# Two transformer blocks in split fp32r on one core: weight blocks woven in pairs and read with a step of two, even and odd tokens as stationary blocks

## The chip, the cores and the metric

The kernel runs on one core of one Trainium2 chip. The metric is device time in microseconds (us) of one execution; it ran three times, in 753.06, 753.13 and 756.38 us, median 753.13 us.

## What is computed

A sequence of 256 tokens of width 1024 goes through two different blocks, all in float32. The first block: an RMS norm and an input projection to 4608 columns, a gated causal convolution with 31 taps and one with 3 taps, two output projections joined by sigmoid gates, a projection back, a feed-forward part (up to 2 x 2816 columns, 3-tap convolution, gelu, product, down to 1024) and a gated embedding branch. The second block: two kinds of attention over 256 tokens, then

```
h = rms_norm(x, ffn_pre_g)
u = h @ w_up                      # 1024 x 8192
c = 3-tap causal convolution of u over tokens, plus bias
g, val = split(c)
o = (gelu(g) * val) @ w_down      # 4096 x 1024
x = x + rms_norm(o, ffn_post_g)
```

Some 134 MB of weights are read from HBM once each.

## The kernel before

**Split products.** Every weight and every activation is held as two fp32r tiles, a rounded part (`hi`) and the rest (`lo`). A product of two of them is three matmuls: hi x hi, lo x hi, hi x lo. Each matmul takes a stationary operand of 128 partitions x 128 columns, which a weight load (PEld in the profile) puts into the array first, and streams a moving operand past it.

**Units.** A weight matrix comes in units of 8 blocks (the first down projection 11, one small projection 4), each block 128 x 128, lying side by side in a partition: block k is `[:, k*P:(k+1)*P]`, 128 adjacent floats. SyncE loads a unit (512 KB, line 564) into one of four `raw` buffers, ScalarE rounds it to `w_hi` (L787), VectorE (L1223) or, for some units, GpSimd (L636) writes `w_lo`, and TensorE consumes it. Buffers rotate with a ring of four; work on a unit is done up to three units ahead. The order on every engine is written out by hand.

**TensorE.** `products` (L1895 to L1906) multiplies all blocks of a unit. Three lines hold nearly all of the work: L1901 (`w_hi` stationary, hi part of the activation moving), L1902 (`w_hi` again, lo part) and L1903 (`w_lo`, hi part). The moving operand is `hi[:, k, :]`, 256 tokens in adjacent floats. `lagging` (L1914, L1915, L1920) and the second input unit (L2017, L2018, L2021) do the same in another order. Each of the three matmuls has a weight load of its own.

The second down projection (`down2`, L2347 to L2349, `token_products`) is the other way round: the stationary operand is a block of 128 tokens of `f_hi` or `f_lo`, and 512 weight columns stream past:

```
to, tok = o_tile(half, b)[:], slice(b * P, (b + 1) * P)
cols = slice(first_col(u) + j * HALF, first_col(u) + (j + 1) * HALF)
wh, wl = (w[slot(u)][:, cols] for w in (w_hi, w_lo))
nc.tensor.matmul(to, f_hi[:, k, tok], wh, start=start, stop=False)
nc.tensor.matmul(to, f_lo[:, k, tok], wh, start=False, stop=False)
return nc.tensor.matmul(to, f_hi[:, k, tok], wl, start=False, stop=stop)
```

`first_col(u)` is 0 for the first three units of `down2` and 8 from the fourth on: from there the weights lie 32 bytes later in their buffers, and nothing else about the matmuls differs.

**Other matmuls.** L2287 and L2293 transpose `X` and `branch` (stationary, 128 x 128) against the identity. L1959 sums squares with one moving column. L2217 to L2220 multiply attention probabilities with 64 moving columns. L2076 streams 256 columns of `ones_over` past blocks of `conv`, in plain float32.

**VectorE in the second up projection** (`up2`, 64 units). For each unit it does `feed_forward`'s share: a scaling of the bank (L1281), two taps of the convolution (L1572), one of L1590 (`src`) and L1562 (`f_lo`) in turn, and the `w_lo` of a later unit, except for every fourth unit, which GpSimd splits.

**The step before `up2`.** `scale_branch` (L1780) multiplies a chunk of `branch`, 128 x 256, by a per-token factor in a PSUM bank, into `tmp`; the sum with `X` follows, and ScalarE squares it (L811) and rounds it (L814).

Of the kernel before, what the change touches and what calls it, by code (L numbers as in the profile page):

```python
# [20 lines left out]
P = 128  # L21
TOK = 256
D = 1024
DC = D // P
# [8 lines left out]
HALF = D // 2  # L33
# [245 lines left out]
def build(nc, d):  # L279
    f32, f32r = mybir.dt.float32, mybir.dt.float32r  # L280
    ALU, ACT, AX = mybir.AluOpType, mybir.ActivationFunctionType, mybir.AxisListType
    ds = bass.ds

    with ExitStack() as ctx:
# [18 lines left out]
        ident = sb("ident", [P, P])  # L303
# [28 lines left out]
        h2_hi, h2_lo = sb("h2_hi", [P, DC, TOK], f32r), sb("h2_lo", [P, DC, TOK], f32r)  # L332
# [108 lines left out]
        def o_tile(half, b):  # L441

            return bank[UP2_BANKS[2 * half + b]]
# [91 lines left out]

        def slot(u):
            return u % RING

        def on_side(u):
            return u - UNIT0["out2"] in OUT2_SIDE  # L540
# [674 lines left out]
        def _(dve):  # L1215
# [561 lines left out]

            def scale_branch(c):

                nc.vector.tensor_tensor(tmp[c % 4][:], branch[:, c, :], rbc[:, 0:TOK], ALU.mult  # L1780
                                        ).then_inc(res_step, 1)

            for c in range(1 + len(OUT2_SIDE), DC - 2):
# [98 lines left out]
        def _(pe):  # L1882
# [7 lines left out]
            def unit_here(u, it=0):  # L1890
                pe.wait_ge(lo_ready[slot(u)], it + (u // RING + 1))

            def products(ps, s, block0, ks, hi, lo, start, stop, ready=None, w=None):

                w_of = w or (w_hi[s], w_lo[s])  # L1895
                for n, k in enumerate(ks):
                    if ready is not None:
                        pe.wait_ge(*ready(k))
                    b = block0 + n
                    wh, wl = (part[:, b * P:(b + 1) * P] for part in w_of)  # L1900
                    nc.tensor.matmul(ps, wh, hi[:, k, :], start=start and n == 0, stop=False)  # L1901
                    nc.tensor.matmul(ps, wh, lo[:, k, :], start=False, stop=False)  # L1902
                    last = nc.tensor.matmul(ps, wl, hi[:, k, :], start=False,  # L1903
                                            stop=stop and n == len(ks) - 1)
                return last

            def lagging(tiles, ks, hi, lo, hi_here, lo_here, start, stop):

                for k in list(ks) + [None]:
                    if k is not None:  # L1910
                        pe.wait_ge(*hi_here(k))
                        for ps, s in tiles:
                            wh, wl = (part[s][:, k * P:(k + 1) * P] for part in (w_hi, w_lo))
                            nc.tensor.matmul(ps, wh, hi[:, k, :], start=start and k == ks[0], stop=False)  # L1914
                            nc.tensor.matmul(ps, wl, hi[:, k, :], start=False, stop=False)  # L1915
                    if k != ks[0]:
                        behind = ks[-1] if k is None else k - 1
                        pe.wait_ge(*lo_here(behind))
                        for ps, s in tiles:
                            last = nc.tensor.matmul(ps, w_hi[s][:, behind * P:(behind + 1) * P],  # L1920
                                                    lo[:, behind, :], start=False,
                                                    stop=stop and k is None)
                            if stop and k is None:
                                last.then_inc(unit_done, 1)
# [13 lines left out]
            def mean_squares(name):  # L1938

                col = ones_over[:, 0:1] if name == "ln" else ones_over[:, P:P + 1]  # L1940
                parts = ["final", "final_g"] if name == "final" else [name]
                chunks = CK if name == "ln" else DC
                sums = (sumsq,) if name in ALL_ADDED or name == "final" else (sumsq, last_sq)
                if name == "in":
                    sums = (sumsq[:, 0:1, :], sumsq[:, 1:2, :])
                    pe.wait_ge(sum_ready, ADD["in", DC - 2])
                elif name == "up2":
                    sums = (sumsq[:, 0:1, :], sumsq[:, 1:2, :])
                    pe.wait_ge(pair_sum, DC // 2 - 1)
                elif name == "final":  # L1950
                    pe.wait_ge(last_added, 1)
                else:
                    pe.wait_ge(sum_ready, ADD[parts[-1], chunks - len(sums)])
                for n in range(len(parts)):
                    for b in range(2):
                        for k, part in enumerate(sums):
                            if part is last_sq and b == 0:
                                pe.wait_ge(sq_ready, SQ[parts[n], chunks - 1])
                            last = nc.tensor.matmul(stat_of(name)[:, 2 * n + b:2 * n + b + 1],  # L1959
                                                    part[:, n, b * P:(b + 1) * P], col,  # L1960
                                                    start=k == 0, stop=k == len(sums) - 1)
                last.then_inc(stat_ready, 1)

# [48 lines left out]
            def rounded_first(u):  # L2012

                ps = in_tile(u)
                for k in range(DC):
                    wh = w_hi[slot(u)][:, k * P:(k + 1) * P]
                    nc.tensor.matmul(ps, wh, h2_hi[:, k, :], start=k == 0, stop=False)  # L2017
                    nc.tensor.matmul(ps, wh, h2_lo[:, k, :], start=False, stop=False)  # L2018
                unit_here(u)
                for k in range(DC):  # L2020
                    last = nc.tensor.matmul(ps, w_lo[slot(u)][:, k * P:(k + 1) * P], h2_hi[:, k, :],  # L2021
                                            start=False, stop=k == DC - 1)
                last.then_inc(unit_done, 1)

            for u in range(24):
# [11 lines left out]
                first = 0  # L2037
# [87 lines left out]
            def down_tile(name, i, t, it, per_tile, ready=None):  # L2125

                k = BLOCKS[name]
                for r in range(per_tile):
                    u = UNIT0[name] + per_tile * i + r
                    unit_here(u, it)  # L2130
                    if r == 0:
                        if isinstance(it, int):
                            bank_free(t)
                        else:
                            bank_free(t, it, 2 if per_tile == 2 else 1)
                    products(bank[slot(t)][:, 0:TOK], slot(u), 0, range(k * r, k * r + k),
                             f_hi, f_lo, r == 0, r == per_tile - 1, ready).then_inc(unit_done, 1)

            for i in range(DC):
                down_tile("down", i, TILE0["down"] + i, 0, 2, chunk_ready("f") if i == 0 else None)  # L2140
# [143 lines left out]
            def x_transposes(b):  # L2284

                for c in range(DC):
                    last = nc.tensor.transpose(xT_ps[b][c // 4][:, c % 4 * P:(c % 4 + 1) * P],  # L2287
                                               X[:, c, b * P:(b + 1) * P], ident[:])
                last.then_inc(xT_done, 1)

            def branch_transposes(b, first, end):
                for c in range(first, end):
                    last = nc.tensor.transpose(branch_ps[b][c // 4][:, c % 4 * P:(c % 4 + 1) * P],  # L2293
                                               branch[:, c, b * P:(b + 1) * P], ident[:])
                if end == DC:
                    last.then_inc(branchT_done, 1)

# [43 lines left out]

            def token_products(half, b, u, j, k, start, stop):

                to, tok = o_tile(half, b)[:], slice(b * P, (b + 1) * P)
                cols = slice(first_col(u) + j * HALF, first_col(u) + (j + 1) * HALF)
                wh, wl = (w[slot(u)][:, cols] for w in (w_hi, w_lo))
                nc.tensor.matmul(to, f_hi[:, k, tok], wh, start=start, stop=False)  # L2347
                nc.tensor.matmul(to, f_lo[:, k, tok], wh, start=False, stop=False)  # L2348
                return nc.tensor.matmul(to, f_hi[:, k, tok], wl, start=False, stop=stop)  # L2349
# [32 lines left out]
def units_of(w, k_blocks, order=None):  # L2382


    K, N = w.shape
    t = w.reshape(K // P, P, N // P, P).transpose(2, 0, 1, 3)
    if order is not None:
        t = t[order]
    t = t.reshape(-1, k_blocks, P, P).transpose(0, 2, 1, 3)
    return t.reshape(-1, P, k_blocks * P)  # L2390


# [69 lines left out]
```

## Time and profile before

| | |
|---|---|
| median of three executions | 753.13 us (753.06 to 756.38) |
| span of the profiled execution | 753.8 us; its page gives no other time of its own |
| TensorE matmul / weight load | 744.0 us (99%) / 723.4 us (96%), 5950 of each |
| VectorE | 577.9 us (77%) |
| ScalarE | 452.2 us (60%) |
| GpSimd | 210.7 us (28%) |
| HBM read | 133.80 MB, 179 GB/s over the span |

Busy times count every instant at which at least one instruction of that engine is under way. Matmuls are pipelined: several are under way at once and their ends are modelled, so the distance between two starts says more than the duration of one. PEld is the weight load, which overlaps the matmul before it. Starts are in us from the start of the span. A row with xN merges N instructions of one line: its second number reaches from the first start to the last end.

### The profile page before, as it was taken

To read this page: it belongs to the slowest core of one execution; us is meant where nothing else is said; L and a number is where in the kernel's file an instruction comes from. 1 tells how busy PE (TensorE), PEld (TensorE's weight loads), DVE (VectorE), ACT (ScalarE), POOL (GpSimd) and SP (SyncE) were. 2 spreads that over 40 slices of the span, in tenths; PEclk is the share of its full clock that TensorE was granted. 3 is DMA by queue.
4 is the path that set the end of the run, shared out by engine and by line. 5 is a ranking of instruction groups with operands and counts; after the bars stand their busy time and mean duration, and the time that the engine had idled before them with its cause. 6 is when DMAs were issued, how large, how long until landed. Compare 5 with 4: busy or idle time off the path is not lost.

```text
span 753.8 us, 16764 instructions
## 1 busy us (share of the span) xinstructions
PE 744.0 (99%) x5950; PEld 723.4 (96%) x5950; DVE 577.9 (77%) x1049; ACT 452.2 (60%) x765; POOL 210.7 (28%) x136
## 2 busy tenths in 40 slices
PE   8999999999999999999999999999999999999997
PEld 8999999999999999999999999899999999988885
DVE  6999977877887887434887794899999999973333
ACT  7645555556665665444765697876766666643431
POOL 0476743460000000343464002422122122212220
PEclk9999999999999999999999999999999999999999
DMA  8575644565555567644443333355565555666551
GB/s 313 177 238 178 196 155 137 188 207 190 189 184 182 191 200 246 204 161 141 163 165 130 124 130 128 107 195 196 195 194 184 182 192 192 205 217 195 184 179 56
DMA packets 37917, 135.48 MB, mean 180 GB/s; under 512 B 4464, under 2 KB 4720, under 8 KB 37872
## 3 DMA queue, kind: packets, MB, share of 16 engines
q1 hardware_dynamic: 37728, 134.86, 54.3%
q8 instruction: 30, 0.49, 0.3%
q14 instruction: 15, 0.12, 0.1%
q10 hardware_dynamic: 144, 0.00, 0.0%
HBM read 133.80 MB, written 1.05 MB: 179 GB/s over the span
## 4 chain that ended last, share of the span: by engine, by line
PE 72%; DVE 5%; ACT 3%; issue 2%; POOL 1%; DMA 1%; DVEq 0%; POOLq 0%; SPq 0%; ACTq 0%
PE bank L1901 20%; PE bank L1903 19%; PE bank L1902 19%; PE bank L2348 4%; PE bank L2347 4%; PE bank L2349 4%; DVE w_lo L1223 2%; ACT w_hi L787 1%; DMA raw<-in_w_o 1%; POOL X L755 1%; PE bank L2176 1%; ACT score L1079 0%; PE bank L2200 0%; DVE sumsq L1813 0%; DVE score L1730 0%
## 5 line engine op out<-in xcount | busy, mean ns | idle before, releaser
L1901 PE MATMUL bank<-h_hi,w_hi 128*128 128x256 f32 x1372 | 386.6, 282 | 1.6 <-DVE h_lo L1235 0.8
L1902 PE MATMUL bank<-h_lo,w_hi 128*128 128x256 f32 x1372 | 383.4, 279 | 0.0
L1903 PE MATMUL bank<-h_hi,w_lo 128*128 128x256 f32 x1372 | 382.6, 279 | 0.0
L787 ACT ACTIVATE w_hi<-raw 128x1024 fp32r<-128x1024 f32 (+2 forms) x243 | 258.6, 1067 | 94.3 <-PE bank L1903 42.4
L1223 DVE TENSOR_TENSOR w_lo<-raw,w_hi 128x1024 fp32r<-128x1024 f32 (+2 forms) x187 | 235.9, 1264 | 88.4 <-ACT w_hi L787 86.4
L1901 PEld LDWEIGHTS bank<-h_hi,w_hi 128*128 128x128 f32 x1372 | 257.8, 188 | 3.2 <-DVE w_lo L1301 1.0
L1902 PEld LDWEIGHTS bank<-h_lo,w_hi 128*128 128x128 f32 x1372 | 257.9, 188 | 0.0
L1903 PEld LDWEIGHTS bank<-h_hi,w_lo 128*128 128x128 f32 x1372 | 257.9, 188 | 0.0
L636 POOL TENSOR_TENSOR w_lo<-raw,w_hi 128x1024 fp32r<-128x1024 f32 (+1 forms) x56 | 139.0, 2485 | 384.8 <-ACT w_hi L787 376.3
L1281 DVE TENSOR_TENSOR bank<-bank,scales 128x256 f32<-128x256 f32 x116 | 49.4, 429 | 27.4 <-PE bank L1903 21.0
L1572 DVE SCALAR_TENSOR_TENSOR cg<-bank,vec,cg 128x255 f32<-128x255 f32 x108 | 51.2, 474 | 0.7 <-ACT cg L1019 0.6
L2347 PE MATMUL bank<-w_hi,f_hi 128*128 128x512 f32 x128 | 49.9, 390 | 0.0
L2349 PE MATMUL bank<-w_lo,f_hi 128*128 128x512 f32 x128 | 49.9, 390 | 0.0
L2348 PE MATMUL bank<-w_hi,f_lo 128*128 128x512 f32 x128 | 49.9, 390 | 0.0
L1901 PE MATMUL bank<-f_hi,w_hi 128*128 128x256 f32 x176 | 49.5, 281 | 0.0
L1902 PE MATMUL bank<-f_lo,w_hi 128*128 128x256 f32 x176 | 49.3, 280 | 0.0
L1903 PE MATMUL bank<-f_hi,w_lo 128*128 128x256 f32 x176 | 48.9, 278 | 0.0
L649 POOL TENSOR_TENSOR sumsq<-sq,sumsq 128x256 f32<-128x256 f32 x33 | 34.3, 1046 | 52.1 <-ACT sq L811 51.6
L1337 DVE SCALAR_TENSOR_TENSOR conv<-bank,vec,conv 128x256 f32<-128x256 f32 x120 | 48.3, 472 | 0.0
L1562 DVE TENSOR_TENSOR f_lo<-src,f_hi 128x256 f32 (+1 forms) x54 | 42.8, 793 | 0.5 <-ACT f_hi L970 0.5
L970 ACT ACTIVATE f_hi<-src 128x256 f32 (+1 forms) x54 | 22.2, 412 | 31.9 <-DVE src L1590 31.9
L1019 ACT ACTIVATE cg<-bank,vec 128x256 f32<-128x256 f32 x54 | 30.6, 566 | 16.7 <-DVE bank L1281 15.2
(235 smaller groups left out, 948.6 us busy)
## 6 DMA issues: line engine op xcount, KB each, us to landing
raw<-in_w_up SPq DMA_DIRECT2D x108, 512.0 KB, 4.2
raw<-in_w_in SPq DMA_DIRECT2D x53, 512.0 KB, 3.9
raw<-in_w_down SPq DMA_DIRECT2D x32, 512.0 KB, 4.2
raw<-in_w_down SPq DMA_DIRECT2D x16, 704.0 KB, 4.1
raw<-in_w_o SPq DMA_DIRECT2D x8, 512.0 KB, 4.6
raw<-in_w_gate SPq DMA_DIRECT2D x8, 512.0 KB, 3.3
raw<-in_w_out SPq DMA_DIRECT2D x8, 512.0 KB, 3.3
raw<-in_w_b_out SPq DMA_DIRECT2D x4, 512.0 KB, 3.5
```

The costliest lines, as they stand in the source:

```text
L636: nc.gpsimd.tensor_tensor(w_lo[s][:, cols], raw[s][:, cols], w_hi[s][:, cols].bitcast(f32), ALU.subtract).then_inc(lo_ready[s], 1)
L787: nc.scalar.activation(hi_of(u)[:, cols], raw[s][:, cols], ACT.Copy).then_inc(hi_ready, 1)
L1223: nc.vector.tensor_tensor(lo_of(u)[:, cols], raw[s][:, cols], hi_of(u)[:, cols].bitcast(f32), ALU.subtract).then_inc(lo_ready[s], 1)
L1281: nc.vector.tensor_tensor(tile, tile, scales[:, 0, :], ALU.mult).then_inc(scaled, 1)
L1337: nc.vector.scalar_tensor_tensor(conv[:, i, :], a_pad[i][:, tap:tap + TOK], w, conv[:, i, :], ALU.mult, ALU.add).then_inc(conv_step, 1)
L1572: nc.vector.scalar_tensor_tensor(c[:, k:TOK], source[:, 0:TOK - k], vcol(w, 3 * col + (2 - k)), c[:, k:TOK], ALU.mult, ALU.add).then_inc(t ...
L1901: nc.tensor.matmul(ps, wh, hi[:, k, :], start=start and n == 0, stop=False)
L1902: nc.tensor.matmul(ps, wh, lo[:, k, :], start=False, stop=False)
L1903: last = nc.tensor.matmul(ps, wl, hi[:, k, :], start=False, stop=stop and n == len(ks) - 1)
L2347: nc.tensor.matmul(to, f_hi[:, k, tok], wh, start=start, stop=False)
L2348: nc.tensor.matmul(to, f_lo[:, k, tok], wh, start=False, stop=False)
L2349: return nc.tensor.matmul(to, f_hi[:, k, tok], wl, start=False, stop=stop)
```

## The change

Three things change, all of them in how data lies and is addressed. (1) On the host, the blocks of a unit are woven in pairs: blocks 2i and 2i+1 share 256 floats, one in the even places, the other in the odd ones. A stationary operand is then read with a step of two floats over 256 of them. The eleventh block of a unit of the first down projection stays as it was. (2) In `down2`, the two stationary token blocks are the even and the odd tokens in place of the first and the last 128, read from `f_hi` and `f_lo` with a step of two; transposes of `X` and `branch` and the sum of squares ahead of them take their tokens alike, `scale_branch` spreads its factor over the tokens in that order, and the host puts the output rows back in order. (3) Nothing else: the number, the order, the waits and the sizes of the instructions are the same on every engine (the listings of both kernels' instruction orders agree row by row but for line numbers: 3639 rows of TensorE, 625 of VectorE, 536 of ScalarE, 122 of GpSimd, 156 of SyncE). The addresses at which buffers begin are the same too.

```
+        def stationary(tile, k, blocks=DC):
+            if k + 1 == blocks and blocks % 2:
+                return tile[:, k * P:(k + 1) * P]
+            first = k // 2 * 2 * P + k % 2
+            return tile[:, first:first + 2 * P - 1:2]
+
+        def tokens_of(b):
+            return slice(b, TOK - 1 + b, 2)
...
-                nc.vector.tensor_tensor(tmp[c % 4][:], branch[:, c, :], rbc[:, 0:TOK], ALU.mult
+                nc.vector.tensor_tensor(tmp[c % 4][:].rearrange("p (t b) -> p t b", b=2),
+                                        branch[:, c, :].rearrange("p (t b) -> p t b", b=2),
+                                        rbc[:, 0:TOK].rearrange("p (b t) -> p t b", b=2), ALU.mult
                                         ).then_inc(res_step, 1)
...
-                    wh, wl = (part[:, b * P:(b + 1) * P] for part in w_of)
+                    wh, wl = (stationary(part, b, blocks) for part in w_of)
                     nc.tensor.matmul(ps, wh, hi[:, k, :], start=start and n == 0, stop=False)
                     nc.tensor.matmul(ps, wh, lo[:, k, :], start=False, stop=False)
...
-                to, tok = o_tile(half, b)[:], slice(b * P, (b + 1) * P)
+                to, tok = o_tile(half, b)[:], tokens_of(b)
                 cols = slice(first_col(u) + j * HALF, first_col(u) + (j + 1) * HALF)
...
     t = t.reshape(-1, k_blocks, P, P).transpose(0, 2, 1, 3)
-    return t.reshape(-1, P, k_blocks * P)
+    count, pairs = t.shape[0], k_blocks // 2
+    woven = t[:, :, :2 * pairs].reshape(count, P, pairs, 2, P).swapaxes(3, 4)
+    return np.concatenate([woven.reshape(count, P, -1), t[:, :, 2 * pairs:].reshape(count, P, k_blocks % 2 * P)], axis=2)
```

`lagging`, the second input unit, the transposes (L2287, L2293) and the sum of squares of the step before `up2` get the same replacement of their stationary slice.

## Rows read from the trace of the kernel before

**Rows 1.** The page: header, busy times, chain that ended last.

```profile
span 753.8 us, 16764 instructions
PE 744.0 (99%) x5950; PEld 723.4 (96%) x5950; DVE 577.9 (77%) x1049; ACT 452.2 (60%) x765; POOL 210.7 (28%) x136
...
PE bank L1901 20%; PE bank L1903 19%; PE bank L1902 19%; PE bank L2348 4%; PE bank L2347 4%; PE bank L2349 4%; DVE w_lo L1223 2%; ACT w_hi L787 1%; DMA raw<-in_w_o 1%; POOL X L755 1%; PE bank L2176 1%; ACT score L1079 0%; PE bank L2200 0%; DVE sumsq L1813 0%; DVE score L1730 0%
```

**Rows 2.** Matmuls in order of time, first up projection, then `up2`: first and last of 31.

```profile
300.20 0.28 PE L1901 MATMUL bank<-f_hi,w_hi 128*128 128x256 f32 x1
...
303.73 0.28 PE L1901 MATMUL bank<-f_hi,w_hi 128*128 128x256 f32 x1
...
600.02 0.28 PE L1902 MATMUL bank<-h_lo,w_hi 128*128 128x256 f32 x1
...
603.52 0.28 PE L1902 MATMUL bank<-h_lo,w_hi 128*128 128x256 f32 x1
```

**Rows 3.** Matmuls of `down2` in order of time, around the fourth unit's first (669.21).

```profile
667.81 0.40 PE L2347 MATMUL bank<-w_hi,f_hi 128*128 128x512 f32 x1
...
669.21 0.40 PE L2347 MATMUL bank<-w_hi,f_hi 128*128 128x512 f32 x1
...
671.93 0.39 PE L2347 MATMUL bank<-w_hi,f_hi 128*128 128x512 f32 x1
```

**Rows 4.** Weight loads in order of time, those of L2076 and of L1959.

```profile
106.78 1.49 PEld L2076 LDWEIGHTS bank<-conv,ones_over 128*128 128x128 f32 x7
...
15.32 0.86 PEld L1959 LDWEIGHTS bank<-ones_over,sumsq 128*128 128x128 f32 x7
```

**Rows 5.** Matmuls in order of time: eight transposes of `X`.

```profile
473.42 1.04 PE L2287 MATMUL bank<-ident,X 128*128 128x128 f32 x8
```

**Rows 6.** Groups by line and shape: counts and mean duration.

```profile
L1901 PE MATMUL bank<-h_hi,w_hi 128*128 128x256 f32 x1372 | 386.6, 282 | 1.6 <-DVE h_lo L1235 0.8 <-DVE h_lo L1524 0.5 <-DVE w_lo L1223 0.2
L1901 PE MATMUL bank<-f_hi,w_hi 128*128 128x256 f32 x176 | 49.5, 281 | 0.0
L2347 PE MATMUL bank<-w_hi,f_hi 128*128 128x512 f32 x128 | 49.9, 390 | 0.0
L2076 PEld LDWEIGHTS bank<-conv,ones_over 128*128 128x128 f32 x8 | 1.4, 190 | 0.2
```

**Rows 7.** Busy time of each engine in stretches (columns as the last query names them).

```profile
core 0: us, PE busy (x) PEld busy (x) DVE busy (x) ACT busy (x) POOL busy (x), PEclk, DMA share, GB/s
550.00:650.00 100.00, 100.00 (x860) 100.00 (x859) 96.65 (x170) 67.26 (x108) 21.68 (x9) 1.00 0.58 193
...
105.00:150.00 45.00, 44.51 (x370) 43.88 (x369) 32.53 (x59) 25.14 (x42) 18.12 (x9) 1.00 0.47 154
385.00:470.00 85.00, 84.71 (x721) 81.75 (x720) 62.25 (x145) 61.16 (x163) 24.09 (x25) 1.00 0.40 134
470.00:494.00 24.00, 22.68 (x190) 21.75 (x189) 17.96 (x33) 20.11 (x40) 11.68 (x11) 1.00 0.39 129
```

**Rows 8.** VectorE in `up2`, in order of time.

```profile
565.81 0.43 DVE L1281 TENSOR_TENSOR bank<-bank,scales 128x256 f32<-128x256 f32 x1
...
568.01 0.48 DVE L1572 SCALAR_TENSOR_TENSOR cg<-bank,vec,cg 128x254 f32<-128x254 f32 x1
568.61 0.43 DVE L1281 TENSOR_TENSOR bank<-bank,scales 128x256 f32<-128x256 f32 x1
...
569.34 1.74 DVE L1562 TENSOR_TENSOR f_lo<-src,f_hi 128x256 f32 x1
...
571.41 0.43 DVE L1281 TENSOR_TENSOR bank<-bank,scales 128x256 f32<-128x256 f32 x1
```

**Rows 9.** Chain of waits between the convolutions and the projection back.

```profile
129.10 5.95 DMA raw<-in_w_o
```

**Rows 10.** VectorE just before `up2`, in order of time.

```profile
481.91 0.41 DVE L1780 TENSOR_TENSOR tmp<-branch,bank 128x256 f32<-128x256 f32 x1
...
482.79 0.41 DVE L1780 TENSOR_TENSOR tmp<-branch,bank 128x256 f32<-128x256 f32 x1
```

More of the change, by code:

```diff
@@ L1891, in unit_here, with products @@
                 pe.wait_ge(lo_ready[slot(u)], it + (u // RING + 1))
-            def products(ps, s, block0, ks, hi, lo, start, stop, ready=None, w=None):
+            def products(ps, s, block0, ks, hi, lo, start, stop, ready=None, w=None, blocks=DC):
                 w_of = w or (w_hi[s], w_lo[s])
@@ L1912, in lagging @@
                         for ps, s in tiles:
-                            wh, wl = (part[s][:, k * P:(k + 1) * P] for part in (w_hi, w_lo))
+                            wh, wl = (stationary(part[s], k) for part in (w_hi, w_lo))
                             nc.tensor.matmul(ps, wh, hi[:, k, :], start=start and k == ks[0], stop=False)
@@ L1919, in lagging @@
                         for ps, s in tiles:
-                            last = nc.tensor.matmul(ps, w_hi[s][:, behind * P:(behind + 1) * P],
+                            last = nc.tensor.matmul(ps, stationary(w_hi[s], behind),
                                                     lo[:, behind, :], start=False,
@@ L1959, in mean_squares @@
                             last = nc.tensor.matmul(stat_of(name)[:, 2 * n + b:2 * n + b + 1],
-                                                    part[:, n, b * P:(b + 1) * P], col,
+                                                    part[:, n, tokens_of(b) if name == "post" else slice(b * P, (b + 1) * P)], col,
                                                     start=k == 0, stop=k == len(sums) - 1)
@@ L2015, in rounded_first @@
                 for k in range(DC):
-                    wh = w_hi[slot(u)][:, k * P:(k + 1) * P]
+                    wh = stationary(w_hi[slot(u)], k)
                     nc.tensor.matmul(ps, wh, h2_hi[:, k, :], start=k == 0, stop=False)
@@ L2020, in rounded_first @@
                 for k in range(DC):
-                    last = nc.tensor.matmul(ps, w_lo[slot(u)][:, k * P:(k + 1) * P], h2_hi[:, k, :],
+                    last = nc.tensor.matmul(ps, stationary(w_lo[slot(u)], k), h2_hi[:, k, :],
                                             start=False, stop=k == DC - 1)
@@ L2136, in down_tile @@
                     products(bank[slot(t)][:, 0:TOK], slot(u), 0, range(k * r, k * r + k),
-                             f_hi, f_lo, r == 0, r == per_tile - 1, ready).then_inc(unit_done, 1)
+                             f_hi, f_lo, r == 0, r == per_tile - 1, ready, blocks=k
+                             ).then_inc(unit_done, 1)
             for i in range(DC):
@@ L2287, in x_transposes @@
                     last = nc.tensor.transpose(xT_ps[b][c // 4][:, c % 4 * P:(c % 4 + 1) * P],
-                                               X[:, c, b * P:(b + 1) * P], ident[:])
+                                               X[:, c, tokens_of(b)], ident[:])
                 last.then_inc(xT_done, 1)
@@ L2293, in branch_transposes @@
                     last = nc.tensor.transpose(branch_ps[b][c // 4][:, c % 4 * P:(c % 4 + 1) * P],
-                                               branch[:, c, b * P:(b + 1) * P], ident[:])
+                                               branch[:, c, tokens_of(b)], ident[:])
                 if end == DC:
@@ L2459 @@
     r = run_bass_kernel_spmd(nc, [{f"in_{k}": v for k, v in arrays.items()}], core_ids=[0])
-    out = r.results[0]["out"].reshape(2, 2, P, HALF).transpose(0, 2, 1, 3)
+    out = r.results[0]["out"].reshape(2, 2, P, HALF).transpose(2, 0, 1, 3)
     return np.ascontiguousarray(out).reshape(1, TOK, D)
```

## The prediction

> **What bounds the kernel now.** I read the page first. TensorE has a matmul under way 99% of the span and a weight load 96% of it, and the chain that ended last lies on L1901 to L1903 and L2347 to L2349 with 70% [rows 1]. The next engine, VectorE, is at 77%. TensorE hardly waits for anyone, so its time is the number of matmuls times the distance between their starts. That distance is what the reader is to look at, in the rows in order of time.
>
> In the first up projection 30 matmuls of 256 columns take 303.73 - 300.20 = 3.53 us, 117.7 ns each; in `up2` they take 3.50 us, 116.7 ns each [rows 2]. In `down2` six matmuls of 512 columns take 1.40 us, 233.3 ns each, up to 669.21, and from there twelve take 2.72 us, 226.7 ns each [rows 3]. [...]
>
> [...]
>
> [...]
>
> [...] The rows show that the distance depends on an address alone, 233.3 against 226.7 ns [rows 3]. [...]
>
> **512 columns.** 384 matmuls, three lines of 128 [rows 6]. [...] I take 216. The first three units are 36 matmuls: 36 x 17.3 = 0.6 us. The other 348 give 348 x 10.7 = 3.7 us. Together 4.3 us.
>
> **256 columns.** Lines L1901 to L1903 hold 1372 + 176 matmuls each of the two large groups [rows 6], and with the smaller groups of the same shape 1692 each; L1914, L1915, L1920 add 44 each and the second input unit 24: 5232 in all. 48 of them (the eleventh blocks) keep their step of one, worth 0.3 us, neglected. About 280 us of the span run at 116.7 ns, 2400 matmuls, and 2832 run at 117.7. To what do they fall? [...] But a load cannot follow the last at any distance: where only one column streams, the loads of L1959 are (0.86 - 0.19)/6 = 0.112 us apart [rows 4]. The transposes' 0.110 is nearly that. I take 111.7, because the loads of the split products are of L1959's kind, not transposes. Gain: 2832 x 6.0 + 2400 x 5.0 = 29.0 us. With 109.7 it would be 2832 x 8.0 + 2400 x 7.0 = 39.5 us. Both ends are kept for the range.
>
> **Does the next engine let it?** In `up2` VectorE is busy 96.65 of 100 us [rows 7]. For a unit it needs, from start to start, 568.01 + 0.40 - 565.81 = 2.6 us and then idles until the bank comes (568.61); in the unit that GpSimd splits, the write of `f_lo` takes 1.74 us beside it and the unit takes 571.41 - 568.61 = 2.80 us without a gap [rows 8]. Four units: 3 x 2.6 + 2.8 = 10.6 us. TensorE needs 4 x 24 x 116.7 = 11.2 us now, 4 x 24 x 111.7 = 10.7 at my value and 10.5 at 109.7. So at 111.7 VectorE just keeps up; at 109.7 it would be the bound and take back 16 x 0.1 = 2 us, and some more for its late start into `up2`. ScalarE (67%) and the DMA engines (58%) have room [rows 7].
>
> **What is given back.** Three stretches are paced by other engines too. From 105 to 150 the chain runs through VectorE and a transfer of `raw<-in_w_o` of 5.95 us [rows 9]; 370 matmuls there [rows 7] would give 2.1 us, and I count half lost, 1.0. From 470 to 494 ScalarE and VectorE feed TensorE chunk by chunk (PE 22.68 of 24 us, 190 matmuls): 1.0 us, all lost. In attention, 385 to 470, 721 matmuls would give 4 us at most; ScalarE and VectorE are at 72 and 73% with serial steps, and I count a third lost, 1.2. The start of the input projection, where split weights are ready less than 1 us ahead, may cost 0.5. Together 3.7 us.
>
> **`scale_branch`.** Its row takes 0.41 us, and eight of them stand in the chain before `up2`, about 0.88 us apart [rows 10]. Now the factor is read from PSUM in two places in turn, and the output is the same size. No row has such a read. It can cost nothing (same elements) or double, 8 x 0.41 = 3.3 us. I take nothing, as nearest to the many rows of two-operand work at about 0.42 us, and keep 3.3. The stepped transposes and sums are 36 matmuls, and I count nothing for them: their loads are hidden in the same way.
>
> **The sum.** 29.0 + 4.3 - 3.7 = 29.6 us. The profiled execution's span is 753.8 us, 0.7 above the median of 753.13, so I take the gain off the median: **723 us**, 4% faster. This case's own range is 715 to 733.
>
> **Rivals.**
>
> *The load has no floor at 111.7.* Then matmuls of 256 columns fall to 109.7 and VectorE bounds `up2`. Gain 39.5 + 4.3 - 2 - 5 (more is lost in the three stretches) = 37 us: 716. For it: the transposes. Chance 0.15.
>
> *Half of the surcharge stays.* [...] Gain (29.0 + 4.3)/2 - 2 = 15: 738. Chance 0.14.
>
> *Nothing moves.* [...] 753, or up to 756 with `scale_branch`. [...] Chance 0.10.
>
> *The load becomes the slower read.* [...] It decides from the point where a stepped load takes over 117 ns; at 125 ns the kernel would need 5232 x 8 = 42 us more. Chance 0.16. [...]
>
> **Chances and range.** The forecast has 0.45. About half a per cent (4 us) is what a measurement of this kernel can tell from no change. Faster by more: 0.45 + 0.15 + 0.14 = 0.74. Within: 0.10. Slower: 0.16. From 708 (the lower rival with nothing lost, 753.1 - 44) to 755 holds the forecast, both other gains and most of no change, 0.81.
>
> **What the changed profile would show.** Starts of the split products 111 to 113 ns apart in both up projections, with no difference left between them; `down2` at 216 ns, the first three units like the rest. PEld about 188 ns per load as before. VectorE near 100% in `up2`, waiting for ScalarE or TensorE hardly at all. The forecast is wrong if the distance stays over 115 ns, if loads take longer than 190 ns, if `down2` gains and the 256-column products don't (then a load's floor decides), or if TensorE shows idle time in `up2` before L1223's `w_lo`.

## The result, and the profile after

The change makes the kernel slower. Four executions took 772.80 to 774.18 us, median **773.65 us**; the kernel before took 753.23 us beside them, so the ratio is 1.026 (95% interval 1.025 to 1.0276). The forecast was 723 us, and its range ended at 755.

The page of the kernel after, header and busy times, stands against [rows 1]:

```profile
span 771.8 us, 16764 instructions
PE 764.1 (99%) x5950; PEld 744.4 (96%) x5950; DVE 578.8 (75%) x1049; ACT 452.3 (59%) x765; POOL 210.0 (27%) x136
```

The span grew by 18.0 us; TensorE grew by 20.1 and its load side by 21.0, with the same 5950 instructions. The busy times of VectorE, ScalarE and GpSimd did not move by a microsecond. TensorE does not wait longer either: its waits were 3.8 us in seven places before and are 1.8 us in two now. So only the distance between two matmuls is left. Here it is in order of time, for the input projection, the first up projection, `up2` and `down2` (start, duration):

```profile
29.73 0.28 PE L1914 MATMUL bank<-h_hi,w_hi 128*128 128x256 f32 x1
...
33.69 0.28 PE L1914 MATMUL bank<-h_hi,w_hi 128*128 128x256 f32 x1
...
299.94 0.28 PE L1914 MATMUL bank<-f_hi,w_hi 128*128 128x256 f32 x1
...
303.93 0.28 PE L1914 MATMUL bank<-f_hi,w_hi 128*128 128x256 f32 x1
...
599.83 0.28 PE L1915 MATMUL bank<-h_lo,w_hi 128*128 128x256 f32 x1
...
603.83 0.28 PE L1915 MATMUL bank<-h_lo,w_hi 128*128 128x256 f32 x1
...
719.98 0.39 PE L2361 MATMUL bank<-w_hi,f_hi 128*128 128x512 f32 x1
...
722.78 0.39 PE L2361 MATMUL bank<-w_hi,f_hi 128*128 128x512 f32 x1
```

The first three pairs lie 33 matmuls apart: 3.96, 3.99 and 4.00 us, 120.0, 120.9 and 121.2 ns each, where [rows 2] had 117.7 and 116.7. The last pair lies 12 apart: 233.3 ns, where [rows 3] had 226.7 from the fourth unit on. That is the whole difference: 5184 stepped matmuls of 256 columns from 117.2 to 120.6 ns (the means over the long stretches before and after) are 17.6 us, and 348 of 512 columns from 226.7 to 233.3 are 2.3 us, together 19.9 of the 20.4 us between the medians.

Groups of the kernel after, by line and shape:

```profile
L1914 PE MATMUL bank<-h_hi,w_hi 128*128 128x256 f32 x1372 | 392.4, 286 | 0.1
L1914 PEld LDWEIGHTS bank<-h_hi,w_hi 128*128 128x128 f32 x1372 | 269.9, 197 | 1.2 <-issue 0.2 <-DVE w_lo L1234 0.2
L1791 DVE TENSOR_TENSOR tmp<-branch,bank 128x256 f32<-128x256 f32 x8 | 3.3, 412 | 1.2 <-PE bank L1984 1.2
```

A load takes 197 ns in place of 188; loads above 190 ns were one of the signs that the prediction had named for itself being wrong. `scale_branch` takes 0.41 us as before [rows 10]. In `up2` VectorE is busy 92.9 of 100 us in place of 96.65 [rows 7]: it had room, and the wait was TensorE's own pace.

### The profile page after: what moved, and what is told of

Same layout as the page of the kernel before. It is cut to its first block, busy times and chain, and to the rows that moved or that the text cites. A ratio compares the mean times of both kernels' runs of the same rounds, so it can differ in the third digit from the quotient of the medians.

```text
span 771.8 us, 16764 instructions
## 1 busy us (share of the span) xinstructions
PE 764.1 (99%) x5950; PEld 744.4 (96%) x5950; DVE 578.8 (75%) x1049; ACT 452.3 (59%) x765; POOL 210.0 (27%) x136
## 4 chain that ended last, share of the span: by engine, by line
PE 95%; POOL 1%; DVE 1%; issue 1%; DMA 1%; ACT 0%; SPq 0%; DVEq 0%; POOLq 0%
PE bank L1914 27%; PE bank L1915 26%; PE bank L1916 26%; PE bank L2362 4%; PE bank L2363 4%; PE bank L2361 4%; PE bank L2190 1%; DMA raw<-in_w_in 1%; POOL X L766 1%; PE bank L2214 1%; PE bank L1972 1%; PE bank L2232 0%; PE bank L2234 0%; PE bank L1927 0%; PE bank L1933 0%
## 5 line engine op out<-in xcount | busy, mean ns | idle before, releaser
L1914 PE MATMUL bank<-h_hi,w_hi 128*128 128x256 f32 x1372 | 392.4, 286 | 0.1
L1915 PE MATMUL bank<-h_lo,w_hi 128*128 128x256 f32 x1372 | 389.5, 284 | 0.0
L1916 PE MATMUL bank<-h_hi,w_lo 128*128 128x256 f32 x1372 | 389.5, 284 | 0.0
L1914 PEld LDWEIGHTS bank<-h_hi,w_hi 128*128 128x128 f32 x1372 | 269.9, 197 | 1.2 <-issue 0.2
L1915 PEld LDWEIGHTS bank<-h_lo,w_hi 128*128 128x128 f32 x1372 | 269.9, 197 | 0.0
L1916 PEld LDWEIGHTS bank<-h_hi,w_lo 128*128 128x128 f32 x1372 | 269.8, 197 | 0.0
L1030 ACT ACTIVATE cv<-bank,vec 128x256 f32<-128x256 f32 x32 | 18.1, 566 | 40.0 <-DVE bank L1292 40.0
```

Of the source, the lines that this page charges most:

```text
L1030: nc.scalar.activation((cg if r == 0 else cv)[q][:], ff_tile(name, n, turn), ACT.Identity, bias=vcol(b, col), scale=vcol(w, 3 * col + 2)). ...
L1916: last = nc.tensor.matmul(ps, wl, hi[:, k, :], start=False, stop=stop and n == len(ks) - 1)
```

## The experiments

That the distances would fall to 111.7 and 216 ns rested on a supposition of the author that no row shows: that the weight load's read and the stream's read hold each other up where they meet, and that equal pace would end the meetings. Below, the surcharge is what a matmul takes above those two values. Against it stood the theory that the load's own read becomes the slow one. A third possibility was that only the position of the two operands counts. The matmuls had to be measured by themselves first.

### Trains of matmuls by themselves: loads_measured, loads_measured_2

These kernels leave the whole computation of the blocks out. Each line issues 48 matmuls back to back, from tiles whose offsets are known to the byte:

```
+ for n in range(48): nc.tensor.matmul(ps[n % 2][:, 0:256], st(n, 2, 0), mv(n, 256), start=True, stop=True)
  # st(n, step, offset): 128 floats of block n % 8; mv(n, columns): the moving operand
```

> Not the model but 30 trains of 48 split-product matmuls on two fp32r tiles (its output is a copy of weights, the block's computation is left out). Theory A (a weight load has a floor of its own that rises with the step, 112 ns at a step of one and 120 ns at two, because the load touches more memory lines): with 64 moving columns, where only the load counts, the distances are 112 ns at step one, 120 ns at step two and more at four; with 256 moving columns step two gives 120 ns at every offset; with 512 step two is 227 to 233 ns. Theory B (the load itself keeps 112 ns, and the two reads collide): with 64 columns steps one and two give the same 112 ns, and with 256 columns step two falls to 112 ns at some of the four offsets. With the moving operand held at one address (step zero) theory B expects no surcharge in either case, theory A 120 ns at step two.

> Again trains of 48 matmuls and no block computation, now with 256-column trains between the short ones to hold the clock. Theory A2 (each of the two reads has a pace limit of its own, set by the 16-byte pieces it touches; a 512-column stream and a stepped load are both at it and each pays its surcharge by itself): with the stream held at one address, 512 columns are about 216 ns apart at step one and step two alike; with the load held at one address or on one block, they stay at 227 to 234 ns. With 128 moving columns the distance is 112 ns at step one, 118 to 120 at two, about 173 at three and 233 at four. Theory B (the surcharge is made by the two reads meeting): holding either read at one address takes it away, 216 ns in all these trains, and 128 columns give 112 ns at steps one and two. The table of offsets of 256-column trains: A2 expects 116 to 120 ns in every cell, no cell at 112.

The distance in a train is (duration of the row - duration of one matmul)/47. One matmul takes 0.22 us with 128 columns, 0.28 with 256 and 0.39 with 512, and 0.40 where its load is slow (steps of four and eight). The rows are rounded to 0.01 us, which makes 0.2 ns of the distance. Matmuls of the first kernel in order of time. 256 columns: L69 has loads with a step of two, L81 to L83 of three, four and eight, L84 loads of one address. 512 columns: L73 a step of one, L77 of two, L85 one address:

```profile
51.51 5.93 PE L69 MATMUL ps<-mov,sta 128*128 128x256 f32 x48
...
74.59 11.06 PE L73 MATMUL ps<-mov,sta 128*128 128x512 f32 x48
...
119.11 11.36 PE L77 MATMUL ps<-mov,sta 128*128 128x512 f32 x48
...
163.68 8.43 PE L81 MATMUL ps<-mov,sta 128*128 128x256 f32 x48
171.94 11.37 PE L82 MATMUL ps<-mov,sta 128*128 128x256 f32 x48
183.15 11.74 PE L83 MATMUL ps<-mov,sta 128*128 128x256 f32 x48
194.73 5.61 PE L84 MATMUL ps<-mov,sta 128*128 128x256 f32 x48
200.18 11.26 PE L85 MATMUL ps<-mov,sta 128*128 128x512 f32 x48
```

Beside 256 columns a load with a step of two costs 120 ns at all four offsets tried (120.0 to 120.9). A step of three costs 173 ns, of four 233, of eight 241: from four on it costs hardly more. Four floats are 16 bytes. With steps of 2, 3, 4 and 8, 128 floats touch 64, 96, 128 and 128 pieces of 16 bytes, and the distances are 1.88, 1.81, 1.82 and 1.89 ns per piece. From a step of two on, the price goes by pieces, not by bytes. With a step of one it does not: 32 pieces take 112 ns at least (below).

The trains of 64 columns that were to separate the theories in this kernel can't do it. TensorE's granted clock was 0.98 while it streamed 64 columns beside loads of step one, and 0.50 in the two trains behind, so that step one and step two ran at different clocks. The train with a step of four took 233 ns there too (L88, 11.37 us for the 48, clock 0.50): half the clock did not slow it.

Matmuls of the second kernel in order of time. 512 columns: L65 and L66 stream one address, L65 with a load step of one and L66 of two, L67 loads one address, L68 loads one block again and again. 256 columns: L69 loads one address; L71 and L72 stream one address, L71 with a load step of one, L72 of two. 128 columns: L73 a step of one, L75 of two:

```profile
29.42 10.66 PE L65 MATMUL ps<-mov,sta 128*128 128x512 f32 x48
39.92 10.66 PE L66 MATMUL ps<-mov,sta 128*128 128x512 f32 x48
50.41 11.15 PE L67 MATMUL ps<-mov,sta 128*128 128x512 f32 x48
61.40 11.07 PE L68 MATMUL ps<-mov,sta 128*128 128x512 f32 x48
72.31 5.76 PE L69 MATMUL ps<-mov,sta 128*128 128x256 f32 x48
...
83.66 5.54 PE L71 MATMUL ps<-mov,sta 128*128 128x256 f32 x48
89.04 5.82 PE L72 MATMUL ps<-mov,sta 128*128 128x256 f32 x48
94.69 5.47 PE L73 MATMUL ps<-mov,sta 128*128 128x128 f32 x48
...
105.73 5.76 PE L75 MATMUL ps<-mov,sta 128*128 128x128 f32 x48
```

The pair L71, L72 separates the theories. The stream reads one address, so that by the supposition nothing is left to meet, and the stepped load still needs 117.9 ns where the plain one needs 111.9. With 128 columns it is the same: 111.7 and 117.9. **A stepped load has a floor of its own at 118 ns.** (The trains of 128 columns with steps of three and four ran in part at a lower granted clock, 0.79 and 0.64, and are left aside.)

The floor is not the whole loss. In the kernel the distance went from 117.2 to 120.6 ns; a floor of 117.9 forbids any gain, but by itself asks for only 0.7 ns more, 3.6 of the 17.6 us. The rest appears only when both reads move: a stepped load takes 120.0 to 120.9 ns beside a real stream and 117.9 beside one address, a plain one 117.2 to 120.0 and 111.9. For 512 columns the floor can't be the cause at all, for it lies 100 ns below the distance. With the stream at one address both steps take the same 218.5 ns (L65, L66); with a real stream, operands level, a step of one takes 227.0 and a step of two 233.4 (L73, L77 above). That is something the two reads do to each other, and no run says what.

The other surprise is the stream. With the load at one address, 512 columns still take 229 to 231 ns (L67 here, L85 above); with the stream at one address they take 218.5. So most of what 512 columns take above the forecast's 216 ns belongs to the stream: 512 adjacent fp32r columns are 128 pieces too, at 1.77 to 1.81 ns each. With 256 columns and the load at one address, 113.4 (L84 above) to 116.6 ns (L69 here) are left.

A last table of the second kernel varies the two offsets in steps of 32 bytes, modulo 128, at 256 columns and a step of one. Level operands take 119.8 to 120.0 ns in all four cases. Operands apart mostly take 117.9 to 118.7, with one exception at 119.8, (stationary 0, moving 96), and one at 113.4, (64, 0). With 512 columns level is the good place, 227.0 to 227.4; apart, they take 229.1 to 234.3 in both kernels. So position counts as well.

So the larger part of the surcharge of 512 columns does not depend on where the load reads, since it stays with the load at one address (229 ns, L67). The rest depends on both reads: the same matmul of 256 columns takes 113.4 to 120.0 ns by position alone, and the step of the load moves the distance of 512 columns by 6 ns (227.0 in L73, 233.4 in L77), though the load's own floor of 118 ns lies far below it.

### The two halves of the change: weights_only, tokens_only

The first kernel keeps the woven weights alone, the second the even and odd tokens alone.

```
weights_only                                      tokens_only
 def tokens_of(b):                                 def stationary(tile, k, blocks=DC):
-    return slice(b, TOK - 1 + b, 2)              -    first = k // 2 * 2 * P + k % 2
+    return slice(b * P, (b + 1) * P)             -    return tile[:, first:first + 2 * P - 1:2]
                                                  +    return tile[:, k * P:(k + 1) * P]
```

> Only the woven weight blocks; token blocks as before. Theory A: 256-column matmuls 120 to 121 ns apart, 512-column ones 227 and 233 as before: 753 + 5232 x 3.4 ns = 771 us. Theory C (the loss comes from the stepped token blocks, transposes and scale_branch, with the weights neutral): 753 us.

> Only even and odd tokens as stationary blocks, weights as before. Theory A: 256-column matmuls 116.7 and 117.7 ns apart as before, 512-column ones 233 ns throughout, 348 x 6.6 ns = 2.3 us more, and some tenths for transposes and scale_branch: 755.5 to 756 us. Theory C: 770 us or more.

`weights_only` took 770.98 us, ratio 1.0235 (1.0221 to 1.0249), and `tokens_only` 755.86 us, 1.0036 (1.0022 to 1.005). 17.7 and 2.6 us make up the 20.4. Matmuls of `down2` in order of time, 12 apart in the first kernel and 9 in the second:

```profile
700.19 0.39 PE L2359 MATMUL bank<-w_hi,f_hi 128*128 128x512 f32 x1
...
702.91 0.39 PE L2359 MATMUL bank<-w_hi,f_hi 128*128 128x512 f32 x1
```

```profile
699.77 0.39 PE L2358 MATMUL bank<-w_hi,f_hi 128*128 128x512 f32 x1
...
701.87 0.39 PE L2358 MATMUL bank<-w_hi,f_hi 128*128 128x512 f32 x1
```

226.7 ns with whole token blocks, 233.3 with stepped ones: each half of the change pays where its own loads are. In `tokens_only` the matmuls of 256 columns lie 116.7 ns apart everywhere, also in the first up projection, where the profiled run of the kernel before had 117.7 [rows 2], though nothing differs there. That ns can come and go without an edit.

### A step of four in the kernel: weights_step4

```
-            first = k // 2 * 2 * P + k % 2
-            return tile[:, first:first + 2 * P - 1:2]
+            first = k // 4 * 4 * P + k % 4
+            return tile[:, first:first + 4 * P - 3:4]
```

> Weight blocks woven in fours, read with a step of four (the last three blocks of a unit of the first down projection with a step of one): 5088 of the 5232 split matmuls of 256 columns. Theory A2: their load takes 233 ns as in the trains with a step of four, so 5088 x (233.3 - 117.2) = 591 us more, about 1344 us. Theory B, equal pace being what counts: a step of four runs twice as fast as the stream, the mirror image of the kernel before, and costs about as much as that one, 753 to 790 us.

It took 1343.1 us, ratio 1.779 (1.774 to 1.784). The token blocks are those of the kernel before. The weights are woven in fours, 5088 of the 5232 matmuls read them so, and the three blocks left over of a unit of eleven keep a step of one. Matmuls in order of time, where such a unit passes from the one to the other:

```profile
566.12 0.40 PE L1913 MATMUL bank<-f_lo,w_hi 128*128 128x256 f32 x1
566.36 0.40 PE L1914 MATMUL bank<-f_hi,w_lo 128*128 128x256 f32 x1
566.59 0.28 PE L1912 MATMUL bank<-f_hi,w_hi 128*128 128x256 f32 x1
566.71 0.28 PE L1913 MATMUL bank<-f_lo,w_hi 128*128 128x256 f32 x1
566.83 0.28 PE L1914 MATMUL bank<-f_hi,w_lo 128*128 128x256 f32 x1
```

235 ns, then 120: the price hangs on the load of each matmul by itself. 5088 x (233.3 - 117.2) = 591 us, and 588 were measured (the kernel before took 754.8 us beside it). By the theory that an unequal pace makes meetings and nothing else counts, a step of four would have cost at most a few dozen us; it is ruled out.

### Position in the kernel: ring_at_0, ring_at_64, step2_ring_at_0

In the kernel before, activations begin 64 bytes and weight buffers 32 bytes past a multiple of 128. These three move buffers and change nothing else (in `ring_at_0`, `o_ms` and `o_rstd` share a tile, and the shift in `down2` is 64 bytes).

```
-RING_PAST = 32
+RING_PAST = 64                                   # ring_at_0; ring_at_64: 0
-        w_hi = [sb(f"w_hi{i}", [P, UNIT_MAX], f32r, past=RING_PAST) for i in range(RING)]
+        w_hi = [sb(f"w_hi{i}", [P, UNIT_MAX], f32r) for i in range(RING)]
...                                               # raw and w_lo alike
+        at[0] += 64                              # ring_at_0 only
```

> The kernel before with its weight buffers 32 bytes lower, at 0 in place of 32 modulo 128 bytes, so that blocks of weights and activations stand 64 bytes apart modulo 128 (before: 96); the weights of the second down projection from its fourth unit on stand level with the tokens as before. The trains found 113.3 ns or 117.8 ns at a distance of 64. Theory A2 with the meeting of reads as a second, smaller term: 113.3 ns wherever the good pattern locks in, down to 753 - 5232 x 3.9 ns = 733 us; if the other locks in, 117.8 ns and 754 to 756 us. A theory without any effect of position: 753 us.

> The kernel before with its weight buffers at 64 modulo 128, level with the activations. All trains at a distance of 0 gave 120.0 ns: 753 + 5232 x 2.8 ns = 768 us by the trains, with the 512-column matmuls at 226.7 ns in all units. Without any effect of position: 753 us.

> The changed kernel (step of two in weights and tokens) with the weight buffers at 0 modulo 128. Theory A2: the stepped load sets 120 ns wherever it stands, 771 to 774 us as without the shift. If the stepped load only lost by standing badly to the stream: 753 us or less.

`ring_at_64` puts both operands level and took 768.81 us, 1.0197 (1.0182 to 1.0212). Its `up2` in order of time, 30 matmuls, 120.0 ns each:

```profile
599.90 0.28 PE L1901 MATMUL bank<-h_hi,w_hi 128*128 128x256 f32 x1
...
603.50 0.28 PE L1901 MATMUL bank<-h_hi,w_hi 128*128 128x256 f32 x1
```

So 32 bytes cost three quarters of what the whole change costs. Position is a real lever, and of the positions measured in the kernel the one before is the best but for those in which 113.3 ns can occur. `ring_at_0` puts the operands 64 bytes apart and missed the 113.3 ns of the trains: its matmuls lie 117.8 ns apart throughout the profiled execution, and it took 757.93 us, 1.0049 (1.0034 to 1.0065); one of nine executions took 753.47. `step2_ring_at_0` is the changed kernel with that position: 773.7 us, 1.0263 (1.0245 to 1.0281), no better than without. Its `up2` runs at 120.0 ns and its first up projection at 121.2 (at 300 us), against 121.2 and 120.9 without the shift. Neither position tried in the kernel, and none of four offsets in the trains, rescues a step of two.

### Can the kernel have the 113.3 ns? loads_measured_3, w64_h0, loads_measured_4, w64_h0_pairs

The trains of loads_measured_3 follow the kernel's order of operands and come after different neighbours; others are in bf16. Those of loads_measured_4 put 1 to 8 matmuls of another kind ahead. Both leave the computation of the blocks out.

```
+ for n in range(48): ... sta[:, 0:1].broadcast_to([P, P]), mv(n, 256) ...            # L70: loads of one address
+ for n in range(48): ... kernel's order, stationary at 64, moving at 0 ...           # L71 (and L69, after 512 columns)
+ for n in range(48): ... sb16[:, n % 8 * P:n % 8 * P + 127 * 2 + 1:2], mb16[...] ... # bf16
```

> Trains of 48 matmuls again, the block's computation left out. First, bf16 operands, half as many bytes per element. Theory A2 (16-byte pieces set the pace of each read, a stream of adjacent fp32r at full speed is at the limit): a bf16 stream of adjacent elements is not, so 512 columns are 216 ns apart, with a moving step of two they touch as many pieces as fp32r and take 227 to 234 ns, and 256 columns with a moving step of four or eight go up as fp32r does at two (230) and no further than about 240. A stepped bf16 load of two stays hidden under 256 columns. If instead the surcharge is a matter of the step itself or of handing over weights, bf16 at step one pays it too and step two costs more at any width. Second, trains in the kernel's own order (same block twice, then the second tile) with the buffers 64 bytes apart, entered from three different trains: if the 113.3 ns seen once can be had by how a train is entered, some of them show it; the kernel with its buffers at 0 says 117.8 ns.

> Trains in the kernel's order, 36 matmuls each, buffers 64 bytes apart in both arrangements; each is entered from twelve 512-column matmuls, which in the last trains led to 117.8 ns, and then one to eight short ones: loads of one address beside 256 or 128 columns, or loads of 128 adjacent floats beside 128 columns. If the pattern is a matter of how a load stands in time to the stream, few of them (one to four) switch a train to 113.3 ns, and it stays there to its end; if it needs a long run-in, all stay at 117.8 ns.

loads_measured_3 in order of time; L69 and L71 are the same train. In bf16, L95 and L96 stream 512 columns with a step of one and of two, L100 and L102 load with a step of two and of four beside 256, L103 streams 256 with a step of four:

```profile
47.71 5.82 PE L69 MATMUL ps<-mov,sta 128*128 128x256 f32 x48
53.36 5.62 PE L70 MATMUL ps<-mov,sta 128*128 128x256 f32 x48
58.82 5.60 PE L71 MATMUL ps<-mov,sta 128*128 128x256 f32 x48
...
207.26 10.53 PE L95 MATMUL ps<-mb,sb 128*128 128x512 bf16 x48
217.63 11.00 PE L96 MATMUL ps<-mb,sb 128*128 128x512 bf16 x48
...
254.87 5.40 PE L100 MATMUL ps<-mb,sb 128*128 128x256 bf16 x48
...
270.47 5.40 PE L102 MATMUL ps<-mb,sb 128*128 128x256 bf16 x48
275.71 11.04 PE L103 MATMUL ps<-mb,sb 128*128 128x256 bf16 x48
```

The same train runs at 117.9 ns after matmuls of 512 columns (L69) and at 113.3 after loads of one address (L71): at 64 bytes apart there are two stable patterns, and what goes before selects one. The bf16 trains confirm the pieces for the stream. 512 columns with a step of two and 256 with a step of four both touch 128 pieces and take 226 and 227 ns; 512 adjacent ones touch 64 and take 216. With a step of eight (L104, 21.86 us for the 48) every column has a piece of its own, 256 in all, and they take about 455 ns, again 1.78 ns each. The expectation had said no more than 240 there and was wrong. (The granted clock fell to a mean of 0.57 in that train. With a step of one 256 bf16 columns take 109.2 ns at a clock of 1.00, which divided by 0.57 would be some 190 ns, an estimate: the clock alone does not make 455.) One thing does not fit: a bf16 load with a step of four touches 64 pieces as well, and costs nothing (109.2 ns, as with a step of one). In loads_measured_4, with stationary at 64 and moving at 0, two, four or eight matmuls of 256 columns with one-address loads ahead sufficed for 113.3 after the first few matmuls of the train (one did not: 117.9). So did two of 128 columns, but neither one nor four of them, and one of 128 columns with a one-address load, but not three. With stationary at 0 and moving at 64 none of these worked, though 48 one-address loads had (113.3 in loads_measured_3).

```
w64_h0                                            w64_h0_pairs, at every 4th or 8th unit
-RING_PAST = 32                                   +if align and n == 0:
+RING_PAST = 64                                   +    one = w_of[0][:, 16:17].broadcast_to([P, P])
+at[0] += 64        # X and what follows to 0     +    for _ in range(2):
-... // 128 * 128 + 64 if dt == f32r else ...     +        nc.tensor.matmul(ps, one, hi[:, k, :], start=True, stop=True)
+... // 128 * 128 if dt == f32r else ...
```

> The kernel before (step of one) with the weight buffers at 64 and the activations at 0 modulo 128 bytes. In the trains this arrangement kept 113.3 ns for as long as it ran when it was entered from a train of 128 columns or of a load of one address, and 117.8 ns when entered from 512-column matmuls. If the norms' short matmuls bring a phase of the kernel into the good pattern, its matmuls are 113.3 ns apart: down to 735 us if all phases get it, about 3 us less per 30 units. If none does, 117.8 ns and 756 to 758 us, like the buffers at 0 with activations at 64. The up projection of the second block would then leave VectorE (96.65% busy now) next to no idle time.

> The kernel before with the weight buffers at 64 and the activations at 0 modulo 128 bytes, and two extra matmuls of 256 columns, whose load reads one address, at the head of every fourth unit or so (every eighth in the second up projection); the bank they write is overwritten. In the last trains two such matmuls switched to 113.3 ns each time. If that holds in the kernel, the 256-column matmuls of the long phases are 113.3 ns apart: 4400 x 3.9 ns = 17 us less, some 35 pairs x 0.23 us = 8 us more, together about 743 us; where TensorE waits for VectorE the pattern is lost until the next pair. If a pair only works after 512-column matmuls, they stay at 117.8 ns and it takes 762 to 766 us.

`w64_h0` took 747.28 to 757.88 us in ten executions, median 756.0, ratio 0.999 (0.996 to 1.003): **inconclusive**, with a spread of 10.6 us where the kernel before has 2 to 3. Its profiled execution, one of the long ones (757.58 us), shows what is at work; no short one was profiled. Matmuls of the input projection in order of time:

```profile
23.91 0.28 PE L1902 MATMUL bank<-h_hi,w_hi 128*128 128x256 f32 x1
...
27.31 0.28 PE L1902 MATMUL bank<-h_hi,w_hi 128*128 128x256 f32 x1
...
36.27 0.28 PE L1903 MATMUL bank<-h_lo,w_hi 128*128 128x256 f32 x1
36.38 0.28 PE L1904 MATMUL bank<-h_hi,w_lo 128*128 128x256 f32 x1
36.50 0.38 PE L1902 MATMUL bank<-h_hi,w_hi 128*128 128x256 f32 x1
36.72 0.28 PE L1903 MATMUL bank<-h_lo,w_hi 128*128 128x256 f32 x1
```

The first two rows are 30 matmuls at 113.3 ns. The good pattern ends in the 0.22 us gap at 36.50, and up to 118 us every undisturbed matmul is 117.8 ns apart. Then it comes back by itself behind two transposes of `rstd` (55 matmuls from 119.53 to 125.76 us, 113.3 ns each), outlives gaps of 0.19 and 0.22 us at 126.78 and 128.28, and ends at 140.7 without a gap, where the matmuls pass from `a_*` to `h_*`. After that only stretches of 1.4 to 2.5 us show it, at 173, 439 and 463 us. So a gap can end it, but need not, and it can end without one. That the short executions hold it for longer is likely and not shown. The pairs of `w64_h0_pairs` were to bring it back and did not: 762.08 us, ratio 1.0104 (1.0085 to 1.0123), 117.8 ns after every pair. In the trains they had followed matmuls of 512 columns, here they followed more of 256; whether that is the reason was not tested. No version tried beats the kernel before reliably.

## Why the prediction was wrong

**What bounds the kernel: right.** TensorE's time is the number of matmuls times their distance, and the result is that product. The counts held (5232 and 384), and neither VectorE nor a transfer came into it.

**What the surcharge is: wrong for the larger part.** The author took it to come from two reads that meet, a supposition. The trains show three parts of a distance. The largest for 512 columns is the fp32r stream by itself, which takes 229 to 231 ns beside a load of one address. For 256 columns the floor of the plain load, 111.7 to 112.0 ns, makes up all but 5 of the 117.2. What is left, 5 ns there and up to 7 ns by position at either width (113.4 to 120.0, 227.0 to 234.3), appears only when both reads move; it may be the meetings, and no run shows how it comes about. L2076, (1.49 - 0.19)/6 = 0.217 us apart, and the transposes, (1.04 - 0.27)/7 = 0.110 [rows 4, 5, 6], were read as cases where equal pace takes the surcharge away. They show no such thing: in the trains plain f32, where one matmul of 256 columns shows as two records, takes 216 ns for each record with a load step of one and of two alike (L93 and L94 of loads_measured, 96 records in 20.90 and 20.88 us). Why the step costs nothing there, no run shows.

**The step that failed** is the assumption that a stepped load keeps the pace of a plain one. The value "I take 111.7" was the plain load's floor (111.7 to 112.0 measured) used for the stepped one, which needs 118 ns, and beside a real stream 120 to 121. With 120.6 in its place the sum reads 5184 x 3.4 + 348 x 6.6 = 20 us *more*. Of the 8.9 ns between 111.7 and 120.6, 6 are the stepped load's own floor; the other 3 appear only beside a real stream. The 109.7 ns at the upper end of the gain is shown by no run either: the shortest distance of 256 fp32r columns in any train is 111.9, with the stream at one address.

**512 columns: wrong.** No run shows the 216 ns for fp32r; only bf16 takes it. The fp32r stream takes 218.5 even from one address, and 227.0 to 234.3 from 512. The stepped load moved it to 233.3, where the forecast had it fall.

**The rival that came**: "The load becomes the slower read", chance 0.16. Its direction and its threshold ("over 117 ns") are what the trains show: a stepped load takes 117.9 ns by itself and 120.0 to 120.9 beside a real stream. Its scale, 8 ns above 117 for 42 us, gives 5232 x 3.6 = 19 us at 120.6, close to the 20.4 measured. It deserved more: no row of the kernel before has a stepped load, and still the forecast had 0.45. L2076 and the transposes say nothing against it, for they are plain f32 beside plain loads. A plain load takes 112 ns, one with a step of two 118, one with a step of four 233; the 6 ns from the first to the second took away what the prediction had hoped to gain.

**Small terms.** `scale_branch` at nothing: right, 412 ns. The transposes at nothing: wrong but small. Transposes of `X` and `branch` in order of time, kernel after:

```profile
482.82 1.13 PE L2301 MATMUL bank<-ident,X 128*128 128x128 f32 x8
...
487.01 1.84 PE L2307 MATMUL bank<-ident,branch 128*128 128x128 f32 x14
```

(1.13 - 0.27)/7 = 0.123 us in place of 0.110 [rows 5], 32 of them, 0.4 us: the same stepped load seen with a third kind of matmul. The stretches where gain was to be "given back" never came to bear. `up2` slowed with TensorE, and VectorE only idled more. The check of VectorE there also holds a slip: the row of L1572 lasts 0.48 us [rows 8], not 0.40, so a unit needs 2.7 us and four of them 10.8, a little over the 10.7 that TensorE was to need. At 111.7 ns VectorE would have been the bound by a hair.

## What to carry to other kernels

Where a matmul's distance lies within a few ns of its weight load's floor (117.2 against 112 ns here), the load's address pattern is on the critical path: 128 adjacent floats cost 112 ns at least, a step of two 118 (120 beside a stream), a step of four 233. Before re-striding an operand that is read by every matmul, time one train of 48 with that stride; it would have decided this case. When a surcharge changes with an address, that shows that addresses matter, but not that they explain all of it: take each operand's addresses away in turn before building on one.

## What the runs showed of the hardware

- **Reads by 16-byte pieces.** Stepped fp32r loads of 64 to 128 pieces take about 1.8 ns per piece (1.81 to 1.89), and so do streams of 128 pieces (226 to 233 ns, fp32r and bf16) and of 256 (bf16, 455 ns). An fp32r stream of 512 adjacent columns is among them: 227 to 233 ns, against 216 in bf16, where it is 64 pieces. Not explained are the bf16 load with a step of four, which costs nothing (109.2 ns), the last 2 to 3 ns of the kernel's stepped loads (120 to 121, against 117.9 with the stream at one address), which are the larger part of its loss, and the 6 ns that a stepped load adds to 512 columns.
- **Relative position modulo 128 bytes.** 256 columns: level 120.0, most offsets 116.7 to 118.7, 64 bytes apart 113.3 or 117.8. 512 columns: level 226.7 to 227.4, most others about 233 (229.1 with stationary at 0, moving at 64). The kernel before has 116.7 and 226.7.
- **Two stable patterns.** At stationary 64, moving 0 the same code runs at 113.3 or 117.8 ns per matmul by what went before it, and was seen to lose the faster one at a gap of 0.22 us, to keep it over another and to lose it with none. 5232 x 4 ns would be some 21 us, an estimate from these two; how to hold it through the waits stays open.
